# Attention pipeline of a two-block transformer kernel: mixing with one more step between normalisation and transposes, and value products placed ahead of transposes

## The chip, the cores and the metric

The kernel runs on one core of a Trainium2 chip. The metric is the device time of one execution in microseconds; the time before is 1549.24 us, the median of three runs (1548.73 to 1551.07).

## The reference

The reference chains two transformer blocks over 256 tokens of width 1024, all in float32. The first block has a forgetting attention ("fox", 8 heads), a stick-breaking attention ("sb"), a cross-attention to 256 memory tokens ("cross", 4 heads of 256) and a mixture of 16 experts. The second block has two layers; each projects the tokens and a context of 256 more, mixes them in four ways, and applies a gated feed-forward network. The mixing is what the change touches:

```python
y_a = window_gqa(qa, ka, va, ka_c, va_c, sink)          # 4 heads, softmax with a sink
y_b = conformer_conv(ub, conv_w, conv_b, ...)           # depthwise convolution, layer norm
y_c = diff_attention_latent(qc, kc, vc, kc_c, vc_c, lam)  # p1 - lam * p2, then a norm per head
y_d = neighbourhood_attn(qd, kd, vd, kd_c, vd_c, rpb)   # 4 heads with a position bias
yx = jnp.concatenate([y_a, y_b, y_c, y_d], axis=-1) @ w_out
```

In layer 0 the context goes through the same four (without mask and bias), in layer 1 it only serves as keys and values. A `w_ada` product (silu(c) @ w_ada) gives the shifts and scales of both layers.

## The kernel before, in words

Five engines run their own programs and meet at semaphores. Dense products split each float32 operand into a high part (`w_hi`, made by ScalarE at L795) and a low part (`w_lo`, by VectorE at L807) and add three products (L818 to L820).

All softmax attentions go through one pipeline over **units**. A unit is a block of 128 queries of one or two heads: `fox_units` (8), `cross_units` (8), `mix_units[0]` (32: C, A, D of the context, then C, A, D of the tokens) and `mix_units[1]` (16: C, A, D of the tokens). Except in cross a unit has two score matrices ("subs") with up to 512 keys. A and D units have two parts (one per head), a C unit has one part, the difference of its two subs; the values of a C pair are multiplied together, at the second of the pair (`now`). A **group** is what shares one output bank: 8 C units, or 4 A or 4 D units.

The pipeline is written out by steps. In step i:

- TensorE (`pe_attention`, L1335): scores of unit i (L1346, extra terms L1351), which wait for the exponentials of two units before, since four score banks are used in turn (three in cross); the turning of a finished ada batch (L967), which waits for a copy by ScalarE (L978); transposes of unit i-2 (L1363) into two banks, which wait for its normalised probabilities; value products of unit i-3 (L1380), which wait for the copies of the turned probabilities, and with the first unit of a group also for the previous group's bank to be emptied; then `fill(i)`: ada products (L952), and planned steps of the norms in the mixing (L1659, L1670, L1712, L1728, L1738).
- ScalarE (`act_attention`, L1384): copies the turned probabilities of unit i-2 to SBUF (L1393), then the exponentials of unit i (L1402), then copies a finished group out (L1470, L1474), then its fill: ada sums, steps of the norms, at three steps near the end a weight's high part (L795).
- VectorE (`dve_attention`, L1413): the maxima of unit i (L1421); the low half of a group that ScalarE has copied out (L1431), one step after ScalarE; the normalisation of unit i-1 (L1439 and L1443, for C L1447 and L1449); its fill, with a weight's low part (L807) at three steps.

Each engine works in program order, so what stands behind a wait waits too. Probabilities lie in four places of 512 columns in `work`, one per sub, used in turn (L626, L627); turned probabilities in four places. `plan_subln` and `plan_layernorm` (L1639, L1697) assign the pieces of the norms to fixed steps; `finish_plan` runs what is planned behind the last step.

Of the kernel before, what the change touches and what calls it, by code (L numbers as in the profile page):

```python
# [15 lines left out]
P = 128  # L16
D = 1024
KC = D // P
S = 256
# [228 lines left out]
def mixer_program(nc, a, out, counts):  # L248
# [39 lines left out]
    with ExitStack() as ctx:  # L288
# [325 lines left out]
        for u, unit in enumerate(all_units):  # L614
# [8 lines left out]
            for p in unit["now"]:  # L623
                unit_of_part[p["p"]] = u
            s_no += len(unit["subs"])
        NP_, NT = 4, 4  # L626
        prob = lambda s: work[:, (s % NP_) * 512:(s % NP_) * 512 + 512]  # L627
        turned_probs = lambda p: work[:, 2048 + p % NT * 512:2560 + p % NT * 512] if p % NT < 2 else prob_turned[:, p % NT - 2, :]
        by_block = lambda p: turned_probs(p).rearrange("p (b q) -> p b q", b=4)
        score_ring = lambda unit: 3 if unit["group"][0] == "cross" else 4  # L630
# [703 lines left out]

        def pe_attention(pe, units, fill):  # L1335

            ring, first = score_ring(units[0]), units[0]["s"][0]
            for i in range(len(units) + 3):
                if i < len(units):
                    unit = units[i]  # L1340
                    for n in range(len(unit["subs"][0]["qk"])):
                        for s, sc in zip(unit["s"], unit["subs"]):
                            if n == 0 and s - first >= ring:
                                pe.wait_ge(*exp_ready.at(s - ring))
                            q, k = sc["qk"][n]
                            last = pe.matmul(score_bank(unit, s)[:, 0:sc["nk"]], q, k, start=n == 0,  # L1346
                                             stop=n == len(sc["qk"]) - 1)
                    for n in range(len(unit["subs"][0]["extra"])):
                        for s, sc in zip(unit["s"], unit["subs"]):
                            left, right, c0, width = sc["extra"][n]  # L1350
                            last = pe.matmul(score_bank(unit, s)[:, c0:c0 + width], left, right, start=False, stop=True,  # L1351
                                             skip_group_check=True)
                    last.then_inc(*scores_ready.mark(unit["u"]))
                pe_ada_turn_left(pe, i - 2)
                if 2 <= i < len(units) + 2:
                    unit = units[i - 2]
                    nb = unit["subs"][0]["nk"] // P
                    for p in unit["parts"]:
                        pe.wait_ge(*probs_ready.at(p["p"]))
                        if p["p"] >= 2:  # L1360
                            pe.wait_ge(*pT_ready.at(p["p"] - 2))
                        for b in range(nb):
                            last = pe.transpose(bank[2 + p["p"] % 2][:, b * P:(b + 1) * P],  # L1363
                                                prob(p["s"])[:, b * P:(b + 1) * P], ident)
                        last.then_inc(*probs_turned.mark(p["p"]))
                if i >= 3 and units[i - 3]["now"]:
                    unit = units[i - 3]
                    g = groups[unit["group"]]
                    pe.wait_ge(*pT_ready.at(unit["now"][-1]["p"]))
                    if g["no"] >= g["banks"]:  # L1370
                        emptied = by_no[g["no"] - g["banks"]]
                        pe.wait_ge(*act_out.at(("group", emptied)))
                        if emptied[0] in ("cross", "A", "D"):
                            pe.wait_ge(*dve_out.at(("group", emptied)))
                    for n in range(len(unit["now"][0]["pv"])):
                        nb = len(unit["now"][0]["pv"][n][1])
                        for b in range(nb):
                            for p in unit["now"]:
                                o, vals = p["pv"][n]
                                last = pe.matmul(o, vals[b], by_block(p["p"])[:, b, :], start=b == 0, stop=b == nb - 1)  # L1380
                    last.then_inc(*pv_done.mark(unit["u"]))
                fill(i)

        def act_attention(act, units, fill=lambda i: None):  # L1384
            for i in range(len(units) + 3):
                if 2 <= i < len(units) + 2:
                    unit = units[i - 2]
                    nk = unit["subs"][0]["nk"]
                    for p in unit["parts"]:
                        act.wait_ge(*probs_turned.at(p["p"]))  # L1390
                        if p["p"] >= NT:
                            act.wait_ge(*pv_done.at(unit_of_part[p["p"] - NT]))
                        act.activation(turned_probs(p["p"])[:, 0:nk], bank[2 + p["p"] % 2][:, 0:nk],  # L1393
                                       ACT.Copy).then_inc(*pT_ready.mark(p["p"]))
                if i < len(units):
                    unit = units[i]
                    act.wait_ge(*negmax_ready.at(unit["u"]))
                    for s, sc in zip(unit["s"], unit["subs"]):
                        if s >= NP_:
                            act.wait_ge(*probs_turned.at(part_of_sub[s - NP_]))  # L1400
                        nk = sc["nk"]
                        last = act.activation(prob(s)[:, 0:nk], score_bank(unit, s)[:, 0:nk], ACT.Exp, bias=nmax(s),  # L1402
                                              accum_out=rsum(s))
                        if "sink" in unit and s == unit["s"][-1]:
                            last = act.activation(esink(unit["s"][0], 2), esink(unit["s"][0], 2), ACT.Exp)
                        last.then_inc(*exp_ready.mark(s))
                if i >= 3 and units[i - 3]["last"]:
                    g = units[i - 3]["group"]
                    act.wait_ge(*pv_done.at(units[i - 3]["u"]))
                    act_group_out(act, g)  # L1410
                fill(i)

        def dve_attention(dve, units, fill=lambda i: None):  # L1413
            own = Step(dve, dve_step)
            for i in range(len(units) + 4):
                if i < len(units):
                    unit = units[i]
                    s0, n, nk = unit["s"][0], len(unit["subs"]), unit["subs"][0]["nk"]
# [5 lines left out]
                        own.ready(dve.tensor_tensor(nmax(s0, n), nmax(s0, n), nsink[:, unit["sink"]], ALU.min))  # L1424
                        ins = dve.tensor_tensor(esink(s0, n), nmax(s0, n), sink[:, unit["sink"]], ALU.add)
                    ins.then_inc(*negmax_ready.mark(unit["u"]))
                if i >= 4 and units[i - 4]["last"] and units[i - 4]["group"][0] in ("cross", "A", "D"):
                    g = units[i - 4]["group"]
                    dve.wait_ge(*act_out.at(("group", g)))
                    hi, lo, o = group_target(g)  # L1430
                    dve.tensor_tensor(lo, o, hi.bitcast(F32), ALU.subtract).then_inc(*dve_out.mark(("group", g)))  # L1431
                if 1 <= i < len(units) + 1:
# [7 lines left out]
                    for p in unit["parts"]:  # L1440
# [4 lines left out]
                        else:  # L1445
# [3 lines left out]
                            dve.scalar_tensor_tensor(out=prob(s)[:, 0:nk], in0=prob(s)[:, 0:nk], scalar=rinv(s),  # L1449
                                                     in1=prob(s + 1)[:, 0:nk], op0=ALU.mult, op1=ALU.add)\  # L1450
                               .then_inc(*probs_ready.mark(p["p"]))
                if i < len(units) + 3:
                    fill(i)

        def group_target(g):
# [241 lines left out]
        def plan_layernorm(l, step):  # L1697

            name, ns = ("ln", l), 2 - l
            x, d = (v[:, :, 0:ns, :].rearrange("p c s t -> p c (s t)") for v in (conv_acc, conv_d))  # L1700
            moment, blocks, end = MIX_MOMENT[:, 0:ns * S], ns * ST, len(mix_units[l]) + 3
            columns = wide_r[:, 0:blocks], wide_t[:, 0:blocks]
            col = lambda n, c: vec[:, 0, VEC_AT[n] + 2 * l + c:VEC_AT[n] + 2 * l + c + 1]
            hi, lo = xn_hi[:, 2:4, 0:ns * S], xn_lo[:, 2:4, 0:ns * S]
# [87 lines left out]

        def finish_plan(l, engine, eng):

            for step in range(len(mix_units[l]) + 3, 60):
                run_plan(l, engine)(eng, step)


# [969 lines left out]
        def _(pe):  # L2768
# [95 lines left out]
            for l in range(LAYERS):  # L2864
# [29 lines left out]
                for step in range(len(mix_units[l]) + 3, 60):  # L2894
                    run_plan(l, "pe")(pe, step)
                for j in range(4):
                    if j == 0:
# [449 lines left out]
```

## Time and profile before

| | before |
|---|---|
| median of the runs | 1549.24 us |
| profiled execution | 1552.3 us |
| its span | 1549.1 us |
| TensorE busy | 1503.9 us (97%) |
| VectorE busy | 883.1 us (57%) |
| ScalarE busy | 710.5 us (46%) |
| instructions | 23631 |

Fox runs from about 100 to 127 us of the span, cross from 248 to 276, the mixing of layer 0 from 633 to 738 and that of layer 1 from 1254.5 to 1317. Idle time of TensorE is what an attention stage can lose or win; a row of the waits names who ended it. Start times in the order of time are from the span's start. A matmul row that holds several instructions gives their number, and in brackets the idle time ahead of the first and its releaser.

### The profile page before, as it was taken

The page shows a single profiled execution, that of the slowest core. Times are in us where ns is not written, and L with a number is a line of the kernel's source. Part 1 is how long each engine was busy: PE and PEld are TensorE (multiplying, and loading weights), DVE is VectorE, ACT ScalarE, POOL GpSimd, SP SyncE. Part 2 cuts the span into 40 slices and gives each one's busy share as a digit, 9 for nine tenths or more (in the row PEclk, how much of TensorE's full clock was granted, in tenths as well). Part 3 has the DMA queues.
Part 4 walks back from the last instruction along what each step waited for, and adds up shares of the span by engine and source line. Part 5 has one row for each costly group of instructions (what it writes and reads, how often), then busy time and mean ns, then how long its engine had stood idle before and what let it go on. Part 6 is the DMA issues. An engine that isn't in the chain of part 4 may idle for free.

```text
span 1549.1 us, 23631 instructions
## 1 busy us (share of the span) xinstructions
PE 1503.9 (97%) x9911; PEld 1271.5 (82%) x9911; DVE 883.1 (57%) x1253; ACT 710.5 (46%) x1073; POOL 133.5 (9%) x157
## 2 busy tenths in 40 slices
PE   8999999999999999998999999999999998999998
PEld 6986997968888788646778888888878966899998
DVE  5633656566778669778363332333247868555554
ACT  5536553446666454567333212212236457443434
POOL 3002000010000346201100000000002400000000
PEclk9999999999999999889999999999999999999999
DMA  9478558598888652501523232323263350555551
GB/s 311 142 248 269 163 179 266 180 296 281 292 286 272 110 177 82 164 1 7 131 82 120 98 104 87 109 82 102 78 183 127 110 163 1 164 190 174 182 177 68
DMA packets 228945, 242.28 MB, mean 156 GB/s; under 512 B 13096, under 2 KB 222472, under 8 KB 228712
## 3 DMA queue, kind: packets, MB, share of 16 engines
q1 hardware_dynamic: 226704, 238.19, 48.2%
q0 software_dynamic: 1600, 2.37, 1.8%
q8 instruction: 78, 1.28, 0.4%
q10 hardware_dynamic: 536, 0.22, 0.1%
q14 instruction: 27, 0.22, 0.0%
HBM read 239.71 MB, written 1.05 MB: 155 GB/s over the span
## 4 chain that ended last, share of the span: by engine, by line
PE 87%; DVE 7%; ACT 3%; DMA 1%; issue 1%; SPq 1%; DVEq 0%; ACTq 0%
PE bank L818 18%; PE bank L820 18%; PE bank L819 18%; PE score_banks L1346 3%; PE bank L1380 2%; PE bank L2003 2%; PE bank L2010 2%; PE bank L2006 2%; PE bank L1363 1%; PE score_banks L952 1%; DVE small L1421 1%; DVE w_lo L807 1%; PE bank L917 1%; PE bank L919 1%; PE bank L918 1%; PE bank L844 1%
## 5 line engine op out<-in xcount | busy, mean ns | idle before, releaser
L807 DVE TENSOR_TENSOR w_lo<-raw,w_hi 128x2048 fp32r<-128x2048 f32 (+1 forms) x143 | 324.5, 2270 | 219.1 <-ACT w_hi L795 218.5
L818 PE MATMUL bank<-xn_hi,w_hi 128*128 128x256 f32 (+1 forms) x1216 | 401.8, 330 | 2.5 <-DVE w_lo L807 1.1
L820 PE MATMUL bank<-xn_hi,w_lo 128*128 128x256 f32 (+1 forms) x1216 | 398.9, 328 | 0.0
L819 PE MATMUL bank<-xn_lo,w_hi 128*128 128x256 f32 (+1 forms) x1216 | 398.9, 328 | 0.0
L795 ACT ACTIVATE w_hi<-raw 128x2048 fp32r<-128x2048 f32 (+1 forms) x143 | 269.6, 1886 | 127.3 <-PE bank L820 76.8
L818 PEld LDWEIGHTS bank<-xn_hi,w_hi 128*128 128x128 f32 x1216 | 231.4, 190 | 24.5 <-issue 2.2
L820 PEld LDWEIGHTS bank<-xn_hi,w_lo 128*128 128x128 f32 x1216 | 231.3, 190 | 20.0
L819 PEld LDWEIGHTS bank<-xn_lo,w_hi 128*128 128x128 f32 x1216 | 231.4, 190 | 19.8
L1850 DVE SCALAR_TENSOR_TENSOR xT<-bank,mod,xT 128x256 f32<-128x256 f32 x96 | 40.6, 478 | 119.7 <-PE bank L820 97.9
L818 PE MATMUL bank<-hid_hi,w_hi 128*128 128x256 f32 (+1 forms) x328 | 107.8, 329 | 0.6 <-DVE hid_lo L1111 0.6
L819 PE MATMUL bank<-hid_lo,w_hi 128*128 128x256 f32 (+1 forms) x328 | 106.9, 326 | 0.0
L820 PE MATMUL bank<-hid_hi,w_lo 128*128 128x256 f32 (+1 forms) x328 | 106.9, 326 | 0.0
L1421 DVE TENSOR_REDUCE small<-score_banks 128x2 f32<-128x1024 f32 (+3 forms) x64 | 57.9, 905 | 71.5 <-PE score_banks L1346 37.4
L1833 ACT ACTIVATE proj<-bank 128x512 f32<-128x512 f32 (+1 forms) x60 | 31.4, 557 | 127.0 <-PE bank L820 113.0
L1909 ACT ACTIVATE hid_hi<-work 128x1024 fp32r<-128x1024 f32 (+1 forms) x22 | 18.6, 847 | 141.8 <-DVE work L1925 141.8
L1402 ACT ACTIVATE work<-score_banks,small 128x512 f32<-128x512 f32 (+2 forms) x120 | 68.8, 583 | 18.4 <-DVE small L1421 11.6
L1630 POOL TENSOR_TENSOR proj<-proj 128x512 f32<-128x512 f32 (+1 forms) x60 | 71.1, 1185 | 57.0 <-ACT proj L1620 53.8
L818 PE MATMUL bank<-w_hi,xn_hi 128*128 128x256 f32 x256 | 73.3, 286 | 0.0
L819 PE MATMUL bank<-w_lo,xn_hi 128*128 128x256 f32 x256 | 72.5, 283 | 0.0
L820 PE MATMUL bank<-w_hi,xn_lo 128*128 128x256 f32 x256 | 72.5, 283 | 0.0
L818 PEld LDWEIGHTS bank<-hid_hi,w_hi 128*128 128x128 f32 x328 | 62.4, 190 | 6.9 <-issue 1.0
L1346 PE MATMUL score_banks<-proj 64*128 64x512 f32 (+5 forms) x256 | 66.0, 565 | 1.6 <-DVE proj L1860 0.9
(472 smaller groups left out, 2664.3 us busy)
## 6 DMA issues: line engine op xcount, KB each, us to landing
raw<-in_w_ada SPq DMA_DIRECT2D x48, 1024.0 KB, 5.7
raw<-in_w_in SPq DMA_DIRECT2D x30, 1024.0 KB, 6.4
raw<-in_w_gate SPq DMA_DIRECT2D x22, 1024.0 KB, 5.4
raw<-in_w_up SPq DMA_DIRECT2D x22, 1024.0 KB, 5.3
raw<-in_w_exp_down SPq DMA_DIRECT2D x16, 1024.0 KB, 5.1
raw<-in_w_down SPq DMA_DIRECT2D x16, 1024.0 KB, 5.3
raw<-in_w_out SPq DMA_DIRECT2D x12, 1024.0 KB, 6.0
raw<-in_w_exp_up SPq DMA_DIRECT2D x10, 1024.0 KB, 8.9
```

Of the source, the lines that this page charges most:

```text
L795: act.activation(high_half(name), raw[:, raw_slot[r], 0:k * cols], ACT.Copy)\
L807: dve.tensor_tensor(w_lo[:, raw_slot[r], 0:k * cols], raw[:, raw_slot[r], 0:k * cols], high_half(name).bitcast(F32), ALU.subtract)\
L818: pe.matmul(o, s_hi, m_hi, start=i == 0, stop=False)
L819: pe.matmul(o, s_hi, m_lo, start=False, stop=False)
L820: last = pe.matmul(o, s_lo, m_hi, start=False, stop=i == n - 1)
L1346: last = pe.matmul(score_bank(unit, s)[:, 0:sc["nk"]], q, k, start=n == 0, stop=n == len(sc["qk"]) - 1)
L1380: last = pe.matmul(o, vals[b], by_block(p["p"])[:, b, :], start=b == 0, stop=b == nb - 1)
L1402: last = act.activation(prob(s)[:, 0:nk], score_bank(unit, s)[:, 0:nk], ACT.Exp, bias=nmax(s), accum_out=rsum(s))
L1421: ins = dve.tensor_reduce(nmax(s0, n), src, AX.X, ALU.max, negate=True)
L1630: pool.tensor_tensor(acc(1), acc(1), term(l, k), ALU.add).then_inc(*term_added.mark((l, k)))
L1833: last = act.activation(dst, src, ACT.Copy, scale=scale)
L1850: last = dve.scalar_tensor_tensor(out=x, in0=src, scalar=mod[:, name[1], g, s:s + 1], in1=x, op0=ALU.mult, op1=ALU.add)
```

## The change

In the mixing, transposes of a unit now stand three steps behind its scores instead of two, and its values four instead of three (`lag_of`); ScalarE's copies and copies out, and VectorE's low halves, move with them. Normalisation keeps its distance of one step. The mixing's probabilities go round six places, the two new ones in `rstd3`, which holds intermediate values of norms and rotations outside the mixing. In all attentions, fox and cross too, TensorE's value products stand ahead of the transposes of the same step. What was planned for the step behind the last of the pipeline moves one step on.

```diff
-        NP_, NT = 4, 4
-        prob = lambda s: work[:, (s % NP_) * 512:(s % NP_) * 512 + 512]
+        NT = 4
+        MIX_FROM = mix_units[0][0]["s"][0]
+        lag_of = lambda units: 2 if units[0]["s"][0] < MIX_FROM else 3
+        prob_ring = lambda s: 4 if s < MIX_FROM else 6
+
+        def prob(s):
+            i = s % prob_ring(s)
+            return work[:, i * 512:i * 512 + 512] if i < 4 else rstd3[:, i - 4, :]
...
-            for i in range(len(units) + 3):
+            for i in range(len(units) + lag + 1):
...
-                if 2 <= i < len(units) + 2:
-                    unit = units[i - 2]
-                    nb = unit["subs"][0]["nk"] // P
...                                    (transposes, moved below the values)
-                if i >= 3 and units[i - 3]["now"]:
-                    unit = units[i - 3]
+                if i > lag and units[i - lag - 1]["now"]:
+                    unit = units[i - lag - 1]
...                                    (values)
+                if lag <= i < len(units) + lag:
+                    unit = units[i - lag]
+                    nb = unit["subs"][0]["nk"] // P
+                    for p in unit["parts"]:
+                        pe.wait_ge(*probs_ready.at(p["p"]))
...                                    (transposes)
                 fill(i)
...                                    (act_attention)
-                if 2 <= i < len(units) + 2:
-                    unit = units[i - 2]
+                if lag <= i < len(units) + lag:
+                    unit = units[i - lag]
...
-                        if s >= NP_:
-                            act.wait_ge(*probs_turned.at(part_of_sub[s - NP_]))
+                        if s >= prob_ring(s):
+                            act.wait_ge(*probs_turned.at(part_of_sub[s - prob_ring(s)]))
...
-                if i >= 3 and units[i - 3]["last"]:
+                if i > lag and units[i - lag - 1]["last"]:
...                                    (dve_attention)
-                if i >= 4 and units[i - 4]["last"] and units[i - 4]["group"][0] in ("cross", "A", "D"):
+                if i > lag + 1 and units[i - lag - 2]["last"] and units[i - lag - 2]["group"][0] in ("cross", "A", "D"):
...
-                if i < len(units) + 3:
+                if i < len(units) + lag + 1:
                     fill(i)
...                                    (plan_layernorm and the two loops behind the last step)
-            moment, blocks, end = MIX_MOMENT[:, 0:ns * S], ns * ST, len(mix_units[l]) + 3
+            moment, blocks, end = MIX_MOMENT[:, 0:ns * S], ns * ST, len(mix_units[l]) + 4
```

## Rows read from the trace of the kernel before

**Rows 1.** Waits of TensorE, whole span: us in total, times, longest.

```profile
PE bank L1363 <- DVE work L1449: 5.7, 8, 1.5
PE bank L1363 <- DVE work L1443: 4.2, 4, 1.5
PE bank L1380 <- DVE xn_lo L1431: 3.2, 3, 1.1
```

**Rows 2.** Stretches: length, busy PE, PEld, DVE, ACT, POOL, then clock, DMA.

```profile
644.30:657.90 13.60, 13.47 (x61) 6.80 (x60) 9.31 (x31) 8.96 (x35) 0.00 (x0) 0.50 0.44 138
670.30:681.80 11.50, 9.01 (x62) 4.42 (x61) 11.25 (x19) 8.56 (x24) 0.00 (x0) 1.00 0.00 1
681.80:692.10 10.30, 10.30 (x50) 5.97 (x50) 7.03 (x12) 5.80 (x15) 0.00 (x0) 0.50 0.01 2
1254.50:1317.20 62.70, 56.31 (x487) 34.97 (x485) 51.34 (x96) 45.66 (x107) 0.00 (x0) 1.00 0.27 85
```

**Rows 3.** Waits of TensorE, 632 to 738 us: the mixing of layer 0.

```profile
PE bank L1363 <- DVE work L1449: 3.7, 5, 1.5
PE bank L1380 <- DVE xn_lo L1431: 2.0, 2, 1.1
PE bank L1363 <- DVE work L1443: 1.9, 2, 1.1
PE bank L967 <- ACT ada_sums L978: 0.5, 1, 0.5
```

**Rows 4.** Waits of TensorE, 670 to 682 us: C units with 512 keys.

```profile
PE bank L1363 <- DVE work L1449: 2.5, 3, 1.5
```

**Rows 5.** Waits of TensorE, 1254 to 1300 us: C and A units, layer 1.

```profile
PE bank L1363 <- DVE work L1443: 2.3, 2, 1.5
PE bank L1363 <- DVE work L1449: 2.0, 3, 0.9
PE bank L1380 <- ACT sq L1470: 0.3, 1, 0.3
PE bank L967 <- ACT ada_sums L978: 0.2, 1, 0.2
```

**Rows 6.** VectorE in order of time, a C unit of layer 1.

```profile
1258.94 0.15 DVE L1439 RECIPROCAL small<-small 128x2 f32<-128x2 f32 x1
...
1260.38 1.22 DVE L1421 TENSOR_REDUCE small<-score_banks 128x2 f32<-128x1024 f32 x1
1261.52 0.15 DVE L1439 RECIPROCAL small<-small 128x2 f32<-128x2 f32 x1
```

**Rows 7.** TensorE in order of time, a C unit of layer 1.

```profile
1270.00 1.13 PE L1346 MATMUL score_banks<-proj 32*128 32x512 f32 x4
1271.52 0.66 PE L1363 MATMUL bank<-cst,work 128*128 128x128 f32 x4 [0.39 <-DVE work L1449]
1272.11 1.09 PE L1380 MATMUL bank<-prob_turned,proj 128*64 128x128 f32 x16
```

**Rows 8.** VectorE in order of time, end of mixing in layer 1.

```profile
1308.90 0.68 DVE L1431 TENSOR_TENSOR xn_lo<-bank,xn_hi 128x512 fp32r<-128x512 f32 x1
...
1310.49 2.28 DVE L807 TENSOR_TENSOR w_lo<-raw,w_hi 128x2048 fp32r<-128x2048 f32 x1
```

**Rows 9.** TensorE in order of time, end of mixing in layer 1.

```profile
1309.73 1.09 PE L1380 MATMUL bank<-work,proj 128*64 128x128 f32 x16 [1.13 <-DVE xn_lo L1431]
1310.62 1.07 PE L1670 MATMUL bank<-cst,small 128*64 128x128 f32 x16
...
1316.11 1.09 PE L1380 MATMUL bank<-prob_turned,proj 128*64 128x128 f32 x16 [0.32 <-ACT prob_turned L1393]
```

**Rows 10.** ScalarE in order of time, last D units of layer 1.

```profile
1304.18 1.09 ACT L1393 ACTIVATE work<-bank 128x512 f32<-128x512 f32 x2 [1.30 <-PE bank L1363]
...
1306.47 0.61 ACT L1474 ACTIVATE xn_hi<-bank 128x512 fp32r<-128x512 f32 x1
1306.95 1.94 ACT L795 ACTIVATE w_hi<-raw 128x2048 fp32r<-128x2048 f32 x1
```

More of the change, by code:

```diff
@@ L1335, in pe_attention @@
         def pe_attention(pe, units, fill):
-            ring, first = score_ring(units[0]), units[0]["s"][0]
-            for i in range(len(units) + 3):
+            ring, first, lag = score_ring(units[0]), units[0]["s"][0], lag_of(units)
+            for i in range(len(units) + lag + 1):
                 if i < len(units):
@@ L1354, in pe_attention @@
                 pe_ada_turn_left(pe, i - 2)
-                if 2 <= i < len(units) + 2:
-                    unit = units[i - 2]
-                    nb = unit["subs"][0]["nk"] // P
[L1358 to L1365, printed above, removed]
-                if i >= 3 and units[i - 3]["now"]:
-                    unit = units[i - 3]
+                if i > lag and units[i - lag - 1]["now"]:
+                    unit = units[i - lag - 1]
                     g = groups[unit["group"]]
@@ L1381, in pe_attention @@
                     last.then_inc(*pv_done.mark(unit["u"]))
+                if lag <= i < len(units) + lag:
[3 more added lines that the diff above has]
+                        pe.wait_ge(*probs_ready.at(p["p"]))
+                        if p["p"] >= 2:
+                            pe.wait_ge(*pT_ready.at(p["p"] - 2))
+                        for b in range(nb):
+                            last = pe.transpose(bank[2 + p["p"] % 2][:, b * P:(b + 1) * P],
+                                                prob(p["s"])[:, b * P:(b + 1) * P], ident)
+                        last.then_inc(*probs_turned.mark(p["p"]))
                 fill(i)
         def act_attention(act, units, fill=lambda i: None):
-            for i in range(len(units) + 3):
-                if 2 <= i < len(units) + 2:
-                    unit = units[i - 2]
+            lag = lag_of(units)
+            for i in range(len(units) + lag + 1):
+                if lag <= i < len(units) + lag:
+                    unit = units[i - lag]
                     nk = unit["subs"][0]["nk"]
@@ L1406, in act_attention @@
                         last.then_inc(*exp_ready.mark(s))
-                if i >= 3 and units[i - 3]["last"]:
-                    g = units[i - 3]["group"]
-                    act.wait_ge(*pv_done.at(units[i - 3]["u"]))
+                if i > lag and units[i - lag - 1]["last"]:
+                    g = units[i - lag - 1]["group"]
+                    act.wait_ge(*pv_done.at(units[i - lag - 1]["u"]))
                     act_group_out(act, g)
@@ L1414, in dve_attention @@
             own = Step(dve, dve_step)
-            for i in range(len(units) + 4):
+            lag = lag_of(units)
+            for i in range(len(units) + lag + 2):
                 if i < len(units):
@@ L1426, in dve_attention @@
                     ins.then_inc(*negmax_ready.mark(unit["u"]))
-                if i >= 4 and units[i - 4]["last"] and units[i - 4]["group"][0] in ("cross", "A", "D"):
-                    g = units[i - 4]["group"]
+                if i > lag + 1 and units[i - lag - 2]["last"] and units[i - lag - 2]["group"][0] in ("cross", "A", "D"):
+                    g = units[i - lag - 2]["group"]
                     dve.wait_ge(*act_out.at(("group", g)))
@@ L1793, in finish_plan @@
         def finish_plan(l, engine, eng):
-            for step in range(len(mix_units[l]) + 3, 60):
+            for step in range(len(mix_units[l]) + 4, 60):
                 run_plan(l, engine)(eng, step)
@@ L2893, in _ @@
                 pe_attention(pe, mix_units[l], fill)
-                for step in range(len(mix_units[l]) + 3, 60):
+                for step in range(len(mix_units[l]) + 4, 60):
                     run_plan(l, "pe")(pe, step)
```

## The prediction

> **What bounds the kernel now.** I read the table of busy times first, then TensorE's waits, then busy times by stretch, then each engine in order of time. TensorE is busy 97% of the span, so what the change can give is TensorE's idle time around attention. Its waits show that [rows 1]: transposes (L1363) wait 5.7 + 4.2 = 9.9 us for VectorE's normalised probabilities (L1449, L1443), all of it in the two mixings: 3.7 + 1.9 = 5.6 us in layer 0 [rows 3], 2.3 + 2.0 = 4.3 us in layer 1 [rows 5]. Value products (L1380) wait 3.2 us for a group's bank to be emptied by L1431.
>
> The stretches [rows 2] show two more things. VectorE and ScalarE are far from idle in the mixing (layer 1: 51.3 and 45.7 of 62.7 us, TensorE 56.3), and from 670.3 to 681.8 VectorE is busy 11.25 of 11.5 us. And TensorE's clock is at its lower level (0.50, 1.2 GHz) for 13.6 and 10.3 us of layer 0. Before the first fall TensorE had idled 0.5 us at L967 [rows 3], before the second 2.5 us in three waits [rows 4].
>
> **What limits a step.** A C unit with 512 keys costs VectorE 2.58 us (reciprocal to reciprocal), of which the maxima of the next unit are 1.14 [rows 6]. It costs TensorE about 1.06 for scores, 0.59 for transposes and half of 1.02 for a pair's values, 2.2 us [rows 7]; what those rows show longer is the tail of the last matmul, which the next one overlaps. So VectorE sets the pace there. In A and D units scores, transposes and values are each 1.0 us or more, over 3.1 us, and TensorE sets it, but at three steps VectorE also has a weight's low half of 2.28 us [rows 8].
>
> The change gives the probabilities a step more to come. It gives the scores none: scores(i) still wait for exp(i-2), since the score banks stay four, two units. What VectorE delays by a unit reaches TensorE by that way instead: maxima late, exponential late, scores late. At L967 and in the values of a new group the distance is the old one too, and TensorE comes to them with less work in between.
>
> **The change part by part.** No instruction is added or removed: the same scores, transposes, copies and values run, in each mixing over one step more. Only waits change, so I sum TensorE's waits before and after.
>
> *Layer 1 up to the last D units.* Before, they are 2.3 + 2.0 + 0.3 + 0.2 = 4.8 us [rows 5]. After, counting from the start of the first scores: four steps of scores 1.06 and ada 1.0 (about as long), a set of transposes and the scores of step 4 bring TensorE to 10.5. With VectorE's 2.58 us per unit, exp(3) ends at 10.95: scores(5) wait 0.45, and end at 12.0. L967 is next, but ada_sums stand behind exp(4) on ScalarE, which ends at 13.5, the copy at 13.85: a wait of 1.9 (before, transposes and values stood ahead of it). In the A units scores(11) wait 0.55 for exp(9) behind a 1.9 us weight copy [rows 10], L1738 0.25 for its rstd, scores(12) 0.7 for exp(10), whose maxima stand behind the 2.28 us weight pass. The values of the first A unit need the C group copied out, which ScalarE does behind exp(11), 1.2 us after TensorE has arrived. Sum 5.05 us: +0.2 us. Ends: -3 if the maxima are never late, +2.
>
> *The end of the mixing, layer 1.* Before, 1.13 us of waiting for the low half and 0.32 for the last copy, 1.45 in all [rows 9]. After, from the end of the last scores: values 1.0, transposes 1.0 and L1670 1.0 bring TensorE to 3.0. ScalarE starts its copies at 1.6 (first part turned), needs 2.3 for them and the exponentials and 0.5 for the group's high half [rows 10]: 4.5. VectorE's maxima, a normalisation and the 2.2 us weight pass end about then, its low half of 0.6 [rows 8] at 5.2. Idle 2.2 us, and no scores are left to lie in it. Then values(13), (14) and (15) each stand directly behind their own transposes. The copy of two parts takes 1.08 us, of which half can lie beside the transposes: 0.65 us idle each with the hand-over, 1.95 in all. 4.15 against 1.45: +2.7 us. Ends: if the copies hide completely +0.7, if each wait is 1.1 us +4.0.
>
> *Layer 0.* The same end: +2.7. L967 with no values ahead of it: +0.5. C to A with 256 keys: the values of the first A unit wait for a copy that ends some 4.3 us after the scores of the step before, TensorE is there after 3.2: +1.1. A to D: the low half is ready 1.95 us after scores end (maxima 1.14, low half 0.6, hand-overs), and the transposes that lay in this wait now stand behind it; before it was 2.0 - 1.1 = 0.9 [rows 3]: +1.05. In the C units with 512 keys VectorE's work is no shorter: two waits of 0.4 and 0.75 in place of 2.5 [rows 4]: -1.35. What is left of the 5.6 us, 3.1, goes, but for A and C to A the waits of layer 1, 2.7, come: -0.4. One wait of 0.2 at the start is in that 3.1 already. Sum +3.6 us. Ends: -2, if every wait on probabilities goes and the ends cost least; +6.
>
> *Values ahead of transposes in fox and cross.* In a full step the copies have scores and ada, over 2 us, to finish in, and exp(i), queued behind copy(i-2) on ScalarE, comes up to 1.0 us later but is wanted two steps later: 0. At the end the last values of fox stand directly behind their transposes: +0.3. In cross the last copy is held by a 1.9 us weight copy anyway: 0. Ends: 0 and +1.5.
>
> *Places of probabilities.* exp(i) would wait for transposes(i-3), which the copy ahead of it on ScalarE has waited for already: 0. The places in rstd3 have no other user in the mixing.
>
> Sum: 0.2 + 2.7 + 3.6 + 0.3 = +6.8 us.
>
> *Clock.* The first slow stretch follows ada steps and C units with thin work, which the new order doesn't fill; I leave it. The second followed idle time that the new order spreads thinner. In its 10.3 us [rows 2] TensorE did what VectorE's pace would allow in about 7.8 (three units of 2.58), so its going is worth 2.5 us; I give that a half, -1.3 us. Forecast +5.5 us. The profiled execution took 1552.3 us (span 1549.1 and 3.2 around); the median of the runs, 1549.24, is 3.1 lower, and the difference is added to it: 1554.7 us.
>
> A rule of the notes speaks for the change. The Trainium skill, "Perfetto Trace Analysis", Optimization Strategy, takes a gap that repeats on the engine that should be saturated as a sign that there may be too few buffers for the next tile. By it the two new places would remove the 9.9 us. Here the trace disagrees for a part: where the gaps repeat, VectorE stands at 11.25 of 11.5 us [rows 2], so what is short is VectorE's time.
>
> **The rivals.** *A, faster.* VectorE's bursts are absorbed: all 9.9 us go, the ends cost their lower 2 x 0.7, boundaries 1, so -7.5 us, 1541.7 us; with both slow stretches shorter, by half of what they cost at most (5 us), 1537. For it: the longest gaps, 1.1 to 1.5 us [rows 3, 5], stand behind single passes of 2.28 us. Against: the same pass delays maxima, and with them the scores two units on. Chance 0.16.
>
> *B, no change.* The 9.9 us go, and new waits at L967 (2.2), at the boundaries (3.1) and the ends (2 x 2.7) take them back: +0.8, 1550.0 us. It holds if scores(i) wait for exp(i-2) less than 1 us per layer. Chance 0.24.
>
> *C, slower as reckoned.* 1552.5 to 1558 us. Chance 0.45.
>
> *D, slower by the clock too.* New idle times of about 2 us, at the ends or at L967 in layer 1, bring the clock to its lower level where it was full. The dense products behind it then run at half speed for a stretch like those seen, 10.3 or 13.6 us, and lose half of it, 5 to 7 us: 1560.5 us. Chance 0.15.
>
> **How the numbers follow.** Faster by over 0.2% (3.1 us, about what the measurement can tell from no change): A, 0.16. Within it: B, 0.24. Slower: C and D, 0.60. The range leaves out most of A and the far part of D: 1545 to 1560.5 us; C alone has 1552.5 to 1558.
>
> **What would show it.** Right: waits of L1363 on L1443 and L1449 nearly gone; new waits of L1346 on L1402; L1380 waiting for copies (L1393) at the ends, some 0.6 us six times, and for L1431 about 2 us three times; L967 waiting near 2 us in layer 1; the counts of instructions unchanged. Wrong: no waits of L1346 on exponentials (A or B), the mixing of layer 1 shorter than its 62.7 us, or slow slices in the clock's row at other places than before.

## The result, and the profile after

The changed kernel takes 1578.7 us (median of 4 runs, 1571.9 to 1579.1) against 1549.7 us for the kernel before on the same chip: ratio 1.0176, 95% interval 1.016 to 1.0191; by the ratio 27 us slower, by the medians 29. The forecast was 1554.7 us, with a range to 1560.5. The direction was right, the size was not. The profiled execution took 1578.85 us (before: 1552.3).

Three lines of the page after: the span, the busy times and the granted clock in 40 slices.

```profile
span 1577.1 us, 23631 instructions
...
PE 1524.7 (97%) x9911; PEld 1280.0 (81%) x9911; DVE 886.8 (56%) x1253; ACT 710.8 (45%) x1073; POOL 133.6 (8%) x157
...
PEclk9999999999999999769999999999999989999999
```

The instruction counts are unchanged, and TensorE is "busy" 20.8 us longer with the same work. The clock's row points to a cause: two slices of the mixing of layer 0 stand at 7 and 6 tenths, and one of layer 1 at 8. Before, two slices stood at 8 and none in layer 1.

TensorE's waits over the whole span after (us in total, times, longest); they answer to [rows 1].

```profile
PE bank L1376 <- DVE xn_lo L1440: 6.7, 3, 2.4
PE bank L974 <- ACT ada_sums L985: 4.1, 4, 1.7
PE bank L1376 <- ACT sq L1479: 4.0, 3, 1.8
PE bank L1376 <- ACT prob_turned L1401: 3.9, 6, 0.7
...
PE bank L1376 <- ACT work L1401: 1.5, 2, 0.7
```

The line numbers moved: L1376 are the values (before L1380), L1386 the transposes (L1363), L1401 ScalarE's copies (L1393), L1440 the low half of a group (L1431), L1479 the copy out of a C group (L1470), L974 the turning of an ada batch (L967). The waits on normalised probabilities, 9.9 us before, are gone. In their place values wait for a group's bank (6.7 + 4.0), for the copies of their own transposes (3.9 + 1.5), and L974 waits 4.1 us. All TensorE waits sum to 46.0 us after and 38.7 before: +7.3. The forecast's sum of waits was +6.8, but it spoke of the attentions alone. There, by TensorE's order of time, the waits grow by 5.8 us: from 8.7 to 10.9 in the mixing of layer 0, from 6.3 to 8.4 in that of layer 1, and by 1.5 in fox and cross.

Of what lies outside, one wait is new, 2.03 us just behind the mixing of layer 0. VectorE, GpSimd and TensorE there, first before, then after:

```profile
740.79 1.22 DVE L1763 TENSOR_TENSOR proj<-proj 128x1024 f32<-128x1024 f32 x1 [1.68 <-ACT proj L1758]
745.71 4.62 POOL L2758 TENSOR_TENSOR aux<-aux,cst 128x2048 f32<-128x2048 f32 x1 [6.78 <-DMA aux<-in_na_rpb]
```

```profile
755.86 4.64 POOL L2767 TENSOR_TENSOR aux<-aux,cst 128x2048 f32<-128x2048 f32 x1 [6.69 <-DMA aux<-in_na_rpb]
756.61 4.96 DVE L1772 TENSOR_TENSOR proj<-proj 128x1024 f32<-128x1024 f32 x1 [1.68 <-ACT proj L1767]
...
763.98 0.50 PE L900 MATMUL bank<-xn_hi,w_hi 128*128 128x512 f32 x1 [2.03 <-DVE xn_lo L1780]
```

VectorE's product for the convolution branch takes 1.22 us where it is over before GpSimd's pass begins, and 4.96 us here, where the two overlap. Of the runs below, e3 (3.77), e8 (3.74) and e9 (4.77) show the same overlap: the three that have the depth and the whole order, as the changed kernel does. All others have 1.22 to 1.23 us and no overlap.

The mixings by stretch: the whole mixing of layer 0, a part of it, the mixing of layer 1 (columns as in [rows 2]).

```profile
636.31:753.49 117.18, 106.27 (x729) 62.06 (x728) 81.53 (x180) 73.21 (x206) 10.14 (x16) 0.81 0.25 54
678.00:706.00 28.00, 28.00 (x98) 13.04 (x100) 16.91 (x27) 14.56 (x39) 0.00 (x0) 0.51 0.00 1
1272.27:1344.48 72.21, 63.87 (x485) 39.32 (x484) 51.18 (x96) 45.64 (x107) 0.00 (x0) 0.91 0.23 74
```

The second row is the heart of it. For 28 us TensorE never idles, VectorE is busy only 16.9 us, and the granted clock is 0.51, the lower level (1.2 GHz). Before, in this place, were 11.5 us in which VectorE set the pace and 10.3 at the lower level [rows 2].

What stood ahead of two stretches at the lower level, in TensorE's order of time:

```profile
662.72 0.66 PE L1376 MATMUL bank<-work 128*64 128x128 f32 x8 [1.80 <-ACT sq L1479]
...
677.32 0.66 PE L1376 MATMUL bank<-work,proj 128*64 128x128 f32 x8 [2.02 <-DVE xn_lo L1440]
```

The trace's clock records show stretches at the lower level from 664.4 us (6.8 long) and from 678.1 (27.3 long), 1.7 and 0.8 us after these waits ended. Others begin at 647.4 (10.2), behind a 1.12 us wait of L974; at 1285.6 (10.2), in a 1.73 us wait of L974; and at 1333.4 (3.4), at the end of a 2.36 us wait. In all the span they sum to 71.6 us, before to 34.6; in the two mixings to 58.0, before to 23.9.

The end of the mixing of layer 1, from the last scores on, answers to [rows 9]:

```profile
1325.71 1.13 PE L1353 MATMUL score_banks<-proj 64*128 64x512 f32 x4
1326.77 1.13 PE L1358 MATMUL score_banks<-aux,cst 128*128 128x256 f32 x4
1327.83 1.09 PE L1376 MATMUL bank<-prob_turned,work 128*64 128x128 f32 x16
1328.85 1.09 PE L1386 MATMUL bank<-cst,rstd 128*128 128x128 f32 x8
1329.88 1.09 PE L1679 MATMUL bank<-cst,small 128*64 128x128 f32 x16
1333.33 1.89 PE L1376 MATMUL bank<-work,proj 128*64 128x128 f32 x16 [2.36 <-DVE xn_lo L1440]
1335.15 1.91 PE L1386 MATMUL bank<-cst,work 128*128 128x128 f32 x8
1337.75 1.09 PE L1376 MATMUL bank<-prob_turned,proj 128*64 128x128 f32 x16 [0.69 <-ACT prob_turned L1401]
1338.77 1.09 PE L1386 MATMUL bank<-cst,work 128*128 128x128 f32 x8
1340.60 1.09 PE L1376 MATMUL bank<-work,proj 128*64 128x128 f32 x16 [0.74 <-ACT work L1401]
1341.63 1.09 PE L1386 MATMUL bank<-cst,rstd 128*128 128x128 f32 x8
1343.46 1.09 PE L1376 MATMUL bank<-prob_turned,proj 128*64 128x128 f32 x16 [0.74 <-ACT prob_turned L1401]
```

Each set of values stands behind its own transposes and waits for the copy. The waits are 2.36 + 0.69 + 0.74 + 0.74 = 4.5 us; the forecast had 2.2 + 1.95. After the long one, values and transposes take 1.9 us where they take 1.09 elsewhere: that is the lower clock.

Stages in the profiled executions, us, from TensorE's order of time. A mixing counts from its first scores to the first dense product behind it.

| | to the first scores of fox | to mixing 0 | mixing 0 | between | mixing 1 | rest | granted clock |
|---|---|---|---|---|---|---|---|
| before | 100.0 | 532.9 | 104.8 | 516.9 | 62.6 | 232.0 | 0.990 |
| changed | 101.1 | 535.2 | 117.2 | 518.8 | 72.2 | 232.6 | 0.978 |
| e1: order alone | 100.8 | 536.7 | 108.2 | 517.8 | 66.7 | 232.6 | 0.986 |
| e2: depth alone | 100.0 | 532.8 | 96.6 | 517.7 | 64.3 | 232.0 | 0.991 |
| e9: changed, idle times filled | 100.6 | 535.2 | 101.4 | 520.0 | 66.7 | 232.7 | 0.995 |
| e10: depth, idle times filled | 102.2 | 532.9 | 94.9 | 516.4 | 61.5 | 232.0 | 0.996 |

Of the 28 us between the two spans the mixings hold 12.4 + 9.6. The profiled executions of e2 (1545.1 us) and e9 (1558.1 us) are the fastest of their kernels, so these rows show them at their best.

### The profile page after: what moved, and what is told of

It is laid out like the page before. It is cut to its first block, busy times and chain, and to the rows that moved or that the text cites. A ratio compares the mean times of both kernels' runs of the same rounds, so it can differ in the third digit from the quotient of the medians.

```text
span 1577.1 us, 23631 instructions
## 1 busy us (share of the span) xinstructions
PE 1524.7 (97%) x9911; PEld 1280.0 (81%) x9911; DVE 886.8 (56%) x1253; ACT 710.8 (45%) x1073; POOL 133.6 (8%) x157
## 4 chain that ended last, share of the span: by engine, by line
PE 87%; DVE 6%; ACT 3%; DMA 1%; issue 1%; SPq 1%; DVEq 0%; ACTq 0%
PE bank L825 18%; PE bank L827 18%; PE bank L826 18%; PE score_banks L1353 3%; PE bank L1376 3%; PE bank L1386 2%; PE bank L2012 2%; PE bank L2019 2%; PE bank L2015 2%; PE score_banks L959 1%; PE bank L924 1%; PE bank L925 1%; PE bank L926 1%; PE bank L850 1%; PE bank L851 1%
## 5 line engine op out<-in xcount | busy, mean ns | idle before, releaser
L1353 PE MATMUL score_banks<-proj 64*128 64x512 f32 (+5 forms) x256 | 74.4, 612 | 2.0 <-DVE proj L1869 0.9
L827 PEld LDWEIGHTS bank<-hid_hi,w_lo 128*128 128x128 f32 x328 | 62.4, 190 | 5.2
```

The lines of the kernel that those rows point to most:

```text
L827: last = pe.matmul(o, s_lo, m_hi, start=False, stop=i == n - 1)
```

## Experiments

**The two halves apart.** e1 has the new order of values and transposes everywhere, but a distance of two steps and four places. e2 has three steps and six places in the mixing, but transposes ahead of values.

```diff
 e1:  lag_of = lambda units: 2        prob_ring = lambda s: 4
 e2:  the block "values" of pe_attention stands behind the block "transposes"
```

> One half of the change alone: values ahead of transposes in each step of all attentions; the mixing keeps its distance of two steps and four places. Theory 1 (three causes of the 29 us: new waits some 6 us, a slightly longer step of TensorE, the rest the clock's lower level brought on by the new waits): waits on group banks grow from 1.1 to about 2 us and the last values of each mixing wait 0.7 us each, but waits for probabilities shrink since transposes come a value product later; a D step of TensorE is 0.1 to 0.15 us longer; slow time of the clock between the 34.5 us of before and the 71.7 of after; 1552 to 1562 us. Rival (the order itself thins TensorE's work and is what brings the clock down): about 1570 to 1578 us with the slow stretches of after.

> The other half alone: the mixing three steps deep with six places, transposes still ahead of values. Theory 1: waits at L967 of 1.1 and 1.7 us stay, waits on group banks are about 1 us as before, the last values are covered by transposes except the very last (0.3 us), waits on probabilities are gone: 1546 to 1553 us, slow time of the clock near the 34.5 us of before. Rival 1 (the depth is what costs, by the added step and by late scores): 1565 us or more. Rival 2 (the depth is a gain spoiled by the order): below 1546 us.

Measured: e1 1564.7 us, ratio 1.0100 (1.0079 to 1.0121). e2 1548.45 us, ratio 1.0014 (0.9988 to 1.0039), 10 runs from 1545.1 to 1562.6. So the order loses (more than the 1552 to 1562 us that Theory 1 had, less than its rival's 1570) and the depth alone makes no difference that can be told in the median. e1 gets the same kinds of waits as the changed kernel, and still some on probabilities (3.3 us at L1386), 47.9 us in all. Its two largest:

```profile
PE bank L1376 <- ACT sq L1479: 7.3, 3, 3.0
PE bank L1376 <- DVE xn_lo L1440: 5.5, 3, 2.0
```

Two waits of the first row, 3.02 us (up to 716.5) and 2.62 us (up to 1299.4), are the longest waits in a mixing of any run, and no stretch at the lower clock stands behind either.

With the depth alone TensorE waits 33.1 us in all, and the mixing of layer 0 is 8.3 us shorter than before, in e2's fastest execution. The mixings of e2:

```profile
632.87:729.42 96.55, 90.71 (x730) 55.99 (x729) 80.65 (x180) 72.23 (x206) 10.11 (x16) 0.95 0.27 62
1247.14:1311.43 64.29, 59.64 (x485) 37.30 (x484) 51.10 (x96) 45.46 (x107) 0.00 (x0) 0.95 0.26 83
```

The halves don't add up. By the ratios the order costs 15.5 us and the depth 2 (its interval holds zero), both together 27: some 10 us more than the sum. In the profiled executions, of which e2's is its fastest, order alone costs 3.4 us in mixing 0 and depth alone gives 8.3, but both together cost 12.4, and this goes with the 27.3 us stretch that neither half has alone.

e2's ten executions show the clock's part by themselves: 1545.1 us at a mean granted clock of 0.991, 1562.6 at 0.978, one program. With two levels, 1 and 0.5, an execution spent twice the missing share of its span at the lower one. A straight line through a kernel's executions gives what a microsecond there goes with: 0.47 us in e2 (10 executions, 28 to 69 us at the lower level), 0.36 in e7 (12, 28 to 72), 0.40 in the changed kernel (only 4), and 0.25 to 0.34 in the kernel before, e4 and e5, where the spread is small.

The trace of e2 also shows a stretch of 3.4 us from 692.1, 22.7 us after the last wait of TensorE over 0.1 us: a single wait is not needed either.

**Filling idle times.** If the lower clock costs the time and idle times bring it, work in them must shorten the kernel. e3 is the changed kernel with products of 128x512 on the identity (results unused) at its long waits, e4 the kernel before with eight of them in two parts of layer 0.

```diff
+KEEPS = ({5: 2, 12: 3, 16: 4, 28: 2, 32: 4, 33: 1, 34: 1, 35: 1}, {5: 3, 12: 2, 16: 4, 17: 1, 18: 1, 19: 1})
...      # step i of a mixing, behind the scores; waits for the bank left out here:
+        pe_keep(pe, bank[2 + p0 % 2][:, :], KEEPS[l].get(i, 0))
```

> The changed kernel with 29 added matmuls of the identity, 128x512 at about 0.47 us, whose results are overwritten: at both L967 waits (2 and 3), ahead of the values that wait for a group's bank (2 to 4) and in the last three steps (1 each). They lie in idle time, so the waits stay as long. Theory 1 (idle gaps bring the clock down, and half of the slow time is lost): slow time falls from 71.7 us towards 35, and the time from 1578 to about 1560 to 1566 us. Rival (the clock has nothing to do with the gaps, or the slow time costs little since VectorE sets the pace): 1576 to 1584 us.

> The kernel before with eight such matmuls in the mixing of layer 0, one ahead of the transposes in steps 4 to 7 and 17 to 20, where TensorE waits and ahead of the two slow stretches of 13.6 and 10.3 us. Theory 1: one or both stretches go or become shorter; each is worth up to about 3 to 5 us, the matmuls cost at most 8 x 0.47 = 3.8 us where they don't fall into a wait: 1543 to 1550 us. Rival (clock unaffected): 1550 to 1553 us.

Measured: e3 1567.99 us (ratio to the kernel before 1.0117, 1.0088 to 1.0146), 10.7 less than the changed kernel, though with more work; no stretch at the lower clock in a mixing. That is above the 1560 to 1566 us expected and below the rival's 1576. e4 1550.9 us (1.0004, 0.9993 to 1.0015), its time at the lower level down from 34.6 to 12.6 us: the clock did as Theory 1 said, the time is that of the rival. The trace also showed a mistake of mine in the size of the filling. Four products in a wait of 2.4 us:

```profile
1318.97 3.70 PE L1234 MATMUL bank<-cst 128*128 128x512 f32 x8
```

A product is two records and takes 0.93 us, not 0.47. e3's 30 products (its expectation says 29) took 28 us for some 18 us of idle time, e4's eight 7.4 us. So e3 understates what the clock costs. e4's 22 us less at the lower level are worth about what it paid, at a third of a microsecond each; that is an estimate.

**Where in the attentions.** e5 has the new order in fox and cross alone. e7 is the changed kernel with transposes ahead of values again where a group's first values stand and behind the last scores of a mixing. e8 is the changed kernel with filling in two waits only.

```diff
 e5:  for part in ((turn, values) if any(units is m for m in mix_units) else (values, turn)): part(i)
 e7:  ((turn, values) if any(units is m for m in mix_units) and (i >= len(units) or i > lag and
         units[i - lag - 1]["group"] != units[i - lag - 2]["group"]) else (values, turn))
 e8:  KEEPS = ({12: 3, 16: 4}, {})
```

> Values ahead of transposes in the fox and cross attentions alone; both mixings as in the kernel before (two steps, four places, transposes ahead). Theory (each attention step of the new order is 0.14 us longer in TensorE's own hand-overs, and the last values of an attention stand directly behind their own transposes): fox from its first scores to the start of stick 29.4 us against 27.6, cross some 0.6 longer, no new slow stretch in the clock: 1552.0 us, +2.4. Rival (the order costs only where it leaves idle times in the mixings): within 0.5 us of the kernel before.

> The changed kernel, with transposes ahead of values only where a step of the mixings starts the values of a new group and in the steps behind the last scores; in all other steps values stay ahead. Theory (the loss comes from waits of 0.7 to 2.4 us at group changes and ends, for which the new order leaves no cover, and from the clock that falls after them): TensorE's waits fall from 46.0 to about 37 us, stretches at the lower clock from 71.6 to about 35 us, 1553 us. Rival (the order costs in every step, through VectorE's and ScalarE's chains): still 1565 us or more.

> The changed kernel with 7 products of 128x512 on the identity (0.47 us each, results unused) in two of its idle times in layer 0, the wait of 1.8 us from C to A (three products) and that of 2.0 us from A to D (four); nothing else. Theory (these two waits bring the clock down for the 6.8 and 27.3 us behind them): both stretches gone, the others as they are, 1568 us, 10 less than the changed kernel. Rival (the clock falls whatever stands in these idle times, for thin work before them): 1578 us with the stretches in place.

e5: 1553.6 us, ratio 1.0023 (1.0012 to 1.0034), so 2 to 5 us from fox and cross. In the profiled execution fox takes 2.1 us more to the start of the next attention (1.8 in the changed kernel), of it a new wait of 0.70 at L974 and 0.53 in place of 0.16 for the last copy. One stretch at the lower level (6.8 us, from 128.1) is new; how often that comes I did not settle. A full step of fox grows by 0.15 us, in hand-overs. The same step before, then after:

```profile
108.62 0.28 PE L1351 MATMUL score_banks<-cst 128*128 128x128 bf16 x2
108.74 0.60 PE L1363 MATMUL bank<-cst,work 128*128 128x128 f32 x4
109.28 0.44 PE L1380 MATMUL bank<-work,proj 128*64 128x128 f32 x4
109.64 1.07 PE L952 MATMUL bank<-raw,cond 128*32 128x256 f32 x16
```

```profile
109.75 0.29 PE L1358 MATMUL score_banks<-cst 128*128 128x128 bf16 x2
109.96 0.44 PE L1376 MATMUL bank<-work,proj 128*64 128x128 f32 x4
110.33 0.66 PE L1386 MATMUL bank<-cst,work 128*128 128x128 f32 x4
110.92 1.07 PE L959 MATMUL bank<-raw,cond 128*32 128x256 f32 x16
```

From the mask product to the next row it is 0.12 us with transposes behind it and 0.21 with values; from transposes to what follows 0.54 and 0.59. A D step, whose extra term is a float32 product, grows from 4.02 to 4.17 us in the same way. A C step with 512 keys, which has no extra term, does not grow (2.24 us in e3, 2.24 with transposes ahead). Cross, which has none either, is 0.5 us longer, which is what its waits grow by.

e7: 1553.9 us, ratio 1.0042 (1.0020 to 1.0064). The order is undone at six steps of layer 0 and four of layer 1 that have both blocks, and that gives back 25 of the 29 us in the median. Its 12 executions fall in two groups: six from 1550.9 to 1552.1 and one at 1555.7 with clocks of 0.986 to 0.991, five from 1561.6 to 1566.3 with 0.977 to 0.981. The median lies between them. The profiled one (1563.9 us) is of the second group; its waits sum to 32.0 us in all, where 37 were expected, and its time at the lower level to 68.5, where 35 was. Its mixing of layer 0 waits only 4.4 us for other engines but runs at 0.81:

```profile
638.79:747.70 108.91, 104.17 (x729) 61.23 (x728) 81.74 (x180) 72.78 (x206) 10.01 (x16) 0.81 0.24 56
```

That contradicts a part of my expectation: few waits do not rule out low-clock stretches, here 17.1 us from 649.2 and 23.9 from 679.9. The first begins near the ada turn's 1.1 us wait, which e7 leaves, the second 1.8 us after a wait of 1.43 us for a copy (up to 678.1), which the changed kernel does not have.

e8: 1567.4 us (1.0113, 1.0092 to 1.0133), 11.3 less than the changed kernel, by 6.5 us of added work in two waits. The place of the 27.3 us stretch, and the mixing of layer 1, which was left alone:

```profile
681.00:708.00 27.00, 26.34 (x185) 14.41 (x184) 23.87 (x42) 21.11 (x54) 0.00 (x0) 1.00 0.01 2
1264.96:1334.54 69.58, 60.90 (x485) 37.74 (x484) 50.89 (x96) 45.55 (x107) 0.00 (x0) 0.95 0.24 76
```

The clock is full, TensorE gets through 185 records in 27 us where 98 took 28, and VectorE is busy 23.9 us in place of 16.9. The same work can be compared too, from the first values of the D group to the second values of the next C group. In the changed kernel (first value row above) it takes from 677.32 to 706.59, 29.3 us, in e8 18.1:

```profile
706.59 1.09 PE L1376 MATMUL bank<-prob_turned,proj 128*64 128x128 f32 x16
```

```profile
681.00 0.66 PE L1387 MATMUL bank<-work,proj 128*64 128x128 f32 x8
...
699.07 1.09 PE L1387 MATMUL bank<-prob_turned,proj 128*64 128x128 f32 x16
```

This is the cleanest single piece of evidence: products that compute nothing, in these two waits alone, and the stretches behind both are gone. All four executions agree (granted clock 0.988 to 0.989, the changed kernel 0.977 to 0.983). Not all of the gain is theirs: of the 10.6 us between the two spans, 8.4 are in mixing 0 and 2.6 in mixing 1, which the edit left alone and whose stretch of 10.2 us is 3.4 long here. The stretch behind the ada turn, left alone too, is 13.7 us in place of 10.2, against "the others as they are". The products also shift all that follows in time; no run shifted it without filling a wait.

**A better version, and the filling cut to size.** e6 is the deeper mixing with transposes ahead and filling at its waits of 1.1 us and more. (It has 13 products, not the 11 its expectation says, at 0.93 us each.) e9 is e3 and e10 is e6, with the filling cut to the waits.

```diff
 e6:   KEEPS = ({5: 2, 12: 2, 16: 2, 32: 2}, {5: 3, 16: 2})
 e9:   KEEPS = ({5: 1, 12: 2, 16: 2, 28: 1, 32: 2, 33: 1, 34: 1, 35: 1}, {5: 2, 12: 1, 16: 2, 17: 1, 18: 1, 19: 1})
 e10:  KEEPS = ({5: 1, 12: 1, 16: 1, 32: 1}, {5: 2, 16: 1})
```

> The new depth and six places with transposes ahead of values as before, and 11 products of 128x512 on the identity (0.47 us each, results unused) put into TensorE's four waits of 1.1 us and more in the mixings (layer 0 at steps 5, 12, 16, 32, layer 1 at steps 5 and 16). Theory (the depth takes the waits on probabilities away, and what is left against it is that its remaining single waits drop the clock in some executions): no stretch at the lower clock in either mixing, 1543 us with a spread under 4 us between executions, where the depth alone gave 1545 to 1563. Rival (the products cost their own time, 5.2 us, since other engines' chains set the pace): 1550 us or more.

> The changed kernel with identity products of 128x512 in its idle times again, but 19 of them in place of 30, each cut to its wait: the traces show that one product is two records and takes 0.93 us, not 0.47, so that 30 of them took 28 us for some 18 us of idle time. Theory (the lower clock costs the changed kernel some 15 to 20 us, and the waits of 0.7 to 2.4 us bring it down): with no stretch at the lower clock in the mixings and no more work than the idle time holds it takes 1568 - 10 = 1558 us; what is left against the kernel before, 8 us, is the waits, now filled, and hand-overs. Rival (other engines' chains set the pace and the surplus of work in the earlier run was hidden): 1567 us as before.

> The deeper mixing with transposes ahead of values and identity products in four waits of layer 0 and two of layer 1, 7 in place of 13 (6.5 us of them in place of 12.1, for 8.3 us of waits). Theory (the surplus lay on the path, and 0.9 us of work in a wait of 1.1 to 1.7 us is enough to keep the clock): no stretch at the lower clock in the mixings, 1543.3 - 4 = 1539.5 us. Rival (the shorter filling leaves idle times that bring the clock down in some executions): median 1543 us or more with a spread of 10 us.

e9: 1561.3 us (1.0077, 1.0062 to 1.0091), 17.4 less than the changed kernel, 3 above the expectation. Its mixings run at full clock and are 101.4 and 66.7 us long:

```profile
635.72:737.10 101.38, 98.56 (x751) 57.80 (x750) 80.83 (x180) 72.46 (x206) 9.94 (x16) 1.00 0.29 63
1257.05:1323.72 66.67, 64.65 (x501) 37.82 (x500) 50.89 (x96) 45.39 (x107) 0.00 (x0) 1.00 0.25 80
```

e6: 1543.3 us (0.9959, 0.9943 to 0.9975), 6 runs within 2.7 us. e10: 1540.7 us (0.9943, 0.9930 to 0.9956), 6 runs from 1539.1 to 1543.8: faster than both kernels, 9 us below the one before. The gain over e2's best execution (1545.1) is small; over its median, 7.7 us, it is steadiness. The mixings of e10:

```profile
635.08:730.00 94.92, 92.53 (x738) 56.81 (x737) 80.43 (x180) 72.28 (x206) 10.13 (x16) 0.98 0.27 64
1246.42:1307.89 61.47, 59.09 (x491) 36.56 (x490) 50.80 (x96) 45.48 (x107) 0.00 (x0) 1.00 0.27 86
```

One stretch of 3.4 us at the lower level was left in a mixing, so the words "no stretch" of the expectation did not hold fully.

## Why the prediction was wrong

**The waits: right, nearly one by one; their sum in part by luck.** The sum was +6.8, measured +5.8 in the attentions and +7.3 over the span, which has the 2.03 us behind the first mixing that no term stood for. Waits on probabilities: forecast nearly gone, gone. L974 in layer 1: 1.9, measured 1.73. C to A: 1.1 for the context of layer 0, measured 1.80, and 1.2 twice for the tokens, measured 1.11 twice. A to D: 1.95, measured 2.02. The low half at the two ends: 2.2 each, measured 2.36 each. Copies at the end: six of 0.65, measured 0.69 to 0.74. Too high was the wait of scores on exponentials in layer 1, 1.7 us over three places, measured 0.30 once (the prediction had named this as what would show it): VectorE's maxima were not as late as a sum of its durations made them. Too low were fox and cross, +0.3 against +1.5.

**The clock: the step that failed.** The forecast says of the second slow stretch that it "followed idle time that the new order spreads thinner", and books -1.3 us. The change removed the short waits in the C units (0.3 to 1.5 us; e2 shows that the depth does this) but put two waits of 1.80 and 2.02 us into layer 0, which the forecast had itself reckoned at 1.1 and 1.95. Then came a 27.3 us stretch in place of the 10.2 us one. With the idle times filled the kernel is 17.4 us faster (e9), with only those two filled 11.3 (e8). Against the kernel before, 37 us more at the lower level (71.6 and 34.6) are worth some 12 us at the 0.32 us each of e9's median (17.4 us for 54.4 fewer) and 17 at the 0.47 of e2's executions. So the term should have been about +12 to +17, not -1.3. The old stretch was priced low too, at 2.5 us: the two sets of C values, scores and transposes and the product of L1712 took 12.0 us there (681.78 to 693.76) and take 7.0 at full clock in e2 (680.84 to 687.89).

**Rival D had the mechanism and a fraction of its price.** "New idle times of about 2 us, at the ends or at L967 in layer 1, bring the clock to its lower level where it was full": this happened, and layer 1, at full clock before, was at 0.91. But D took one extra stretch of at most 13.6 us, from the longest seen before, and a chance of 0.15. At the places that D names, in layer 1, 13.6 us came (10.2 and 3.4), about what it says; the rest of the 37 us more came mostly in layer 0, behind the wait from A to D. The error in method was to bound a stretch by the longest one in the trace of before, when nothing in that trace said what ends one.

**The rest.** The two spans differ by 28.0 us. Waits 7.3 and clock 12 to 17 leave 4 to 9. The hand-overs, which the forecast did not have, are 0.15 us in a step with an extra term; if all 24 such steps pay it (8 of fox, 16 of A and D of the tokens), that is 3.6 at most. Up to 5 us stay unexplained. Values ahead of transposes in fox and cross stood at +0.3, where e5 measured 2 to 5. That the two halves were priced together hid the main point: the 9.9 us of waits were the depth's to win, and the end effects, boundaries and hand-overs were the order's to lose. With the depth alone, TensorE's waits fall by 5.6 us, of it 3.2 in the mixings.

**Too few buffers.** The forecast set the rule of the Trainium skill ("Perfetto Trace Analysis", Optimization Strategy), by which a repeated gap can mean too few buffers, mostly aside. The trace of e2 agrees with it for these gaps: with the depth alone the 9.9 us of waits on probabilities are gone. Others came, so that the waits in the mixings fall only from 14.9 to 11.7 us; mixing 0 went from 104.8 to 96.6 us in e2's fastest execution, the median not clearly. VectorE at 11.25 of 11.5 us [rows 2] was a short piece, and over the whole mixing of layer 0 it is busy 81 of 105 us.

**What stays open.** Why the lower level lasted 27.3 us at one place and 3.4 at others, why waits of 3.0 us had none behind them, and why one program (e2, e7) falls into it in some executions only. That e9 and e8 shorten the kernel through the clock and not in another way rests on the windows and clock rows; filling also shifts the other engines a little, which I could not separate. No run took filling out of e10 at a single wait, and none kept GpSimd's pass off VectorE's.

## What to carry to other kernels

When a change moves idle time of TensorE, don't only sum it: list the single idle times of more than a microsecond that it makes, and what dense work stands behind each, since the clock may charge several times the wait. Price the two halves of a compound change apart; here the deeper pipeline was worth having and the order was not, because transposes were the cover for the copies and the group's copy out. If a long wait can't be removed, a little useless work in it, cut to less than the wait, can pay; measure its own duration first.

## What the runs showed of the hardware

- Stretches at the lower clock began within 2 us of single idle times of 1.12 to 2.36 us (five in the changed kernel), but such an idle time is neither enough nor needed. In mixing 0 of the changed kernel the waits of 1.11 us (725) and 2.36 us (743) had none behind them, nor had those of 3.02 and 2.62 us in e1; in e2 and e10 a stretch of 3.4 us began 22.7 and 23.4 us after the last wait over 0.1 us.
- A microsecond at the lower level cost between a third and a half of a microsecond here. From the changed kernel to e9 it fell from 71.6 to 17.2 us, and the time by 17.4 in the median (0.32 each) and by 20.7 in the profiled executions (0.38); to e8 by 31.5 for 11.3 (0.36) and 10.7 (0.34). Between executions of one program it was 0.36 (e7) and 0.47 (e2). The Trainium skill ("TensorE: Matmul & The Clock Gate", Terms) puts the penalty at throttled time times one minus the clock ratio, a half; an estimate by that rule is 27 us for e9. The runs gave less. A reason may be that part of the time lies where TensorE would have waited anyway, and the filling adds work of its own; this was not separated.
- Transposes and values of equal size are not free to swap behind an extra product of the scores: 0.15 us a step (fox, D); without one a C step stayed at 2.24 us.
- While GpSimd's 4.6 us pass over 128x2048 ran, VectorE's product of 128x1024 float32 did not end. It took 3.7 to 5.0 us in place of 1.22 and ended 1.1 us after GpSimd's pass, in all four traces that have the two at the same time (changed kernel, e3, e8, e9).
